# Second half of a fused decoder's attention: one visit of ScalarE for both query tiles of a head

## The chip, the cores and the metric

The kernel runs on one core of one Trainium2 chip. The metric is the device time of one execution in microseconds (us). The kernel before takes 2956.78 us, the median of three runs (2955.54 to 2959.35).

## The reference, cut to what matters

A two-layer decoder trunk over 512 tokens of width 1024. Layer 0 mixes gated linear attention and a dilated attention of 8 heads; layer 1 mixes by a recurrent block; after each mixer comes a mixture of 16384 one-neuron experts, of which every token takes 128. All is float32.

```
def reference(x, ...):
    h = x
    for layer in range(2):
        hn = rms_norm(h, mix_norm[layer])
        h = h + (gla_dilated_mixer(hn, ...) if layer == 0 else rglru_mixer(hn, ...))
        hn = rms_norm(h, ffn_norm[layer])
        h = h + peer_ffn(hn, ...)          # 128 rows of u and of v gathered for each token
    return rms_norm(h, final_norm)
```

The dilated attention of a head is computed as one masked softmax: the scores of the query rows over all keys up to them, plus a bias table that holds the penalties of the three branches, then exponentials, their sum, and the product with V, divided by the sum.

## The kernel before, in words

The 512 tokens are worked in two halves of 256, and the experts in eight passes p of 128 tokens (four for each layer). A pass has 128 slots k, one for each expert of a token. In slot k GpSimd issues one gather (1 MB: for each of 128 tokens an 8 KB row that holds u and v) into one of seven ring buffers (`pool`, L279); VectorE multiplies the u half by the token's row and sums it (`dot`, L296); ScalarE takes the Gelu of it (L301), weighs it by the gate (L309) and writes it on a diagonal (`place`, L313, three buffers); TensorE multiplies the diagonal by the v half and adds it up in PSUM (`sum_rows`, L346). Only then is the ring buffer free for the gather seven slots on.

Every other piece of work is spread over the slots by hand: each engine's program is a loop over k, and at the slots named there it issues, behind its own expert work of that slot, the instructions of the mixers, of the choice of the experts of the next pass, and so on. Engines execute in program order, so a piece that waits holds up everything behind it on its engine.

The second half's attention (g=1, called tile 1 here) lies in pass 1, from slot 4 (`ATT_AT`) to slot 42. It has 16 units u: head h = u // 2, query tile tl = u % 2; the even unit has 384 keys, the odd one 512. A unit goes through: scores on TensorE (L744, bank x % 2); bias and row maximum on VectorE (L955), then its scaled negative (L959); exponentials on ScalarE (L843); transposes of the 128-column blocks on TensorE (L752, 3 or 4 of them, one bank); their copy to SBUF on ScalarE (`keep`, L853, two buffers pT); the product with V on TensorE (L760); the reciprocal and the scaled result on VectorE (L963, L966). Before, one unit starts in every second slot: TensorE has the scores of u, the transposes of u-1 and the product of u-2 in slot 4+2u; VectorE has the bias of u and the result of u-2 in slot 8+2u; ScalarE has the exponentials of u and the keep of u-1 in slot 8+2u. The Gelu of the slots and the exponentials use different function tables of ScalarE, and a table is loaded (ACT_TABLE_LOAD) wherever the one follows the other. `Copy`, which the keep, the gates and the diagonals use, needs none.

Other work in these slots: the experts' choice on VectorE (L150 to L230) between slots 12 and 30, and bias tables of 256 KB loaded by SyncE (L641), one for each head into two buffers. The output projection of the mixer starts in slot 50 (`OUT_AT`), with its transposes in slot 46. The other half's attention (g=0) runs before the experts with the same functions.

Of the kernel before, what the change touches and what calls it, by code (L numbers as in the profile page):

```python
# [11 lines left out]
ALU = mybir.AluOpType  # L12
# [3 lines left out]
P = 128  # L16
D = 1024
KD = D // P
T = 512
# [7 lines left out]
GV_W = GH * GDV  # L27
# [529 lines left out]
class First:  # L557
# [170 lines left out]
    def sums(self, g):  # L728
        return self.ps[:, 3 if g else 7, 0:AHD]

    def att_pe(self, pe, g, u):

        nc, n = self.nc, 2 * AH
        if u == 0 and g:
            pe.wait_ge(self.gla_done, g + 1)
            pe.wait_ge(self.w.taken, self.FIRST[g] + self.IN)
        if u in (0, AH):
            pe.wait_ge(self.w.taken, self.until(g, 5 if u else 2))
        if u < n:
            h, tl, t, x = self.unit(g, u)  # L740
            r = slice(AHD * (h % 2), AHD * (h % 2) + AHD)
            if u >= 1 + g:
                pe.wait_ge(self.biased, x - g)
            nc.tensor.matmul(self.raw(g, x, t), self.aq[r, h // 2, tl * P:(tl + 1) * P],  # L744
                             self.ak[r, h // 2, 0:(t + 1) * P], start=True, stop=True).then_inc(self.qk_done, 1)
        if 1 <= u <= n:
            h, tl, t, x = self.unit(g, u - 1)
            pe.wait_ge(self.prob, x + 1)
            if u - 1 >= 1:
                pe.wait_ge(self.kept, x)  # L750
            for k in range(t + 1):
                last = nc.tensor.transpose(self.turned(g, x, t)[:, k * P:(k + 1) * P], self.pr[:, x % 2, k * P:(k + 1) * P], self.ident[:])  # L752
            last.then_inc(self.p_turned, 1)
        if u >= 2:
            h, tl, t, x = self.unit(g, u - 2)
            pe.wait_ge(self.kept, x + 1)
            if u > 2:
                pe.wait_ge(self.av_taken, x)
            for k in range(t + 1):
                last = nc.tensor.matmul(self.sums(g), self.pT[:, x % 2, k * P:(k + 1) * P],  # L760
                                        self.av[:, k, h * AHD:(h + 1) * AHD], start=k == 0, stop=k == t)
            last.then_inc(self.av_done, 1)
# [181 lines left out]

    def att_dve(self, dve, g, u):

        nc, scale = self.nc, float(AHD) ** -0.5
        if u < 2 * AH:
            h, tl, t, x = self.unit(g, u)
            w = (t + 1) * P  # L950
            dve.wait_ge(self.bias_in[h % 2], 16 * (g * AH // 2 + h // 2 + 1))
            dve.wait_ge(self.qk_done, x + 1)
            if u >= 2:
                dve.wait_ge(self.prob, x - 1)
            nc.vector.tensor_tensor_reduce(out=self.sc[:, x % 2, 0:w], in0=self.raw(g, x, t), in1=self.bias[:, h % 2, T - w:T],  # L955
                                           scale=1.0, scalar=NEG, op0=ALU.add, op1=ALU.max,
                                           accum_out=self.mx[:, x:x + 1]).then_inc(self.biased, 1)
            dve.wait_ge(self.biased, x + 1)
            nc.vector.tensor_scalar(self.nb[:, x:x + 1], self.mx[:, x:x + 1], -scale, None, ALU.mult).then_inc(self.neg, 1)  # L959
        if u >= 2:  # L960
            h, tl, t, x = self.unit(g, u - 2)
            dve.wait_ge(self.prob, x + 1)
            nc.vector.reciprocal(self.rden[:, x:x + 1], self.den[:, x:x + 1]).then_inc(self.recip, 1)  # L963
            dve.wait_ge(self.recip, x + 1)
            dve.wait_ge(self.av_done, x + 1)
# [292 lines left out]
ATT_AT = 4  # L1258
# [543 lines left out]
```

## Time and profile before

| | us |
|---|---|
| three runs, median | 2956.78 |
| profiled execution, its own time | 2957.95 |
| profiled execution, span from the first to the last instruction | 2956.2 |
| DMA, mean rate over the span | 400 GB/s |
| VectorE busy | 65% |
| ScalarE busy | 44% |
| TensorE matmul busy | 76% |
| mean granted TensorE clock | 0.852 |

The profile of one execution gives a page (busy time of the engines, the span in 40 slices, the DMA queues, the chain of work that ended last, the costliest groups of instructions) and answers to queries: a timeline of one engine, busy time in chosen stretches, groups of instructions with what ended the idle time before them. In a timeline a row is: start in us, length in us, engine, line of the kernel, operation, written and read tiles with shapes, count of merged instructions, and in brackets the idle time before it and who ended it.

### The profile page before, as it was taken

Reading aid. Unit: us, or ns where it says so; the run is one execution under the profiler, and the core shown is the slowest. Engines: PE = TensorE matmul, PEld = TensorE weight load, DVE = VectorE, ACT = ScalarE, POOL = GpSimd, SP = SyncE. Lnnn points to the kernel's source line nnn. Section 1 sums busy time; section 2 is a strip of 40 time slices with the busy share of each in tenths; the row PEclk is TensorE's granted clock in tenths of the full one; section 3 lists DMA queues with packets and bytes.
Section 4 is the critical chain, followed back from the end, with each engine's and each line's share of the span. In section 5 each row is a group of like instructions: output and inputs, shape, how many; then the busy total and the mean of one; then the engine's idle time right before and its main releaser. Section 6 shows DMA issues by size and latency. Waiting matters only on the chain.

```text
span 2956.2 us, 36171 instructions
## 1 busy us (share of the span) xinstructions
PE 2250.5 (76%) x12024; PEld 885.4 (30%) x12024; DVE 1908.4 (65%) x5677; ACT 1287.1 (44%) x3747; POOL 986.7 (33%) x1028
## 2 busy tenths in 40 slices
PE   8998898788896767778886776878787666756766
PEld 6773343233342222223332221323333111111110
DVE  1247757777477867576578666667478666567444
ACT  3233534485345438334343538433434333335333
POOL 0013333333333333333333333333333333333332
PEclk9999999889997988988998888979998766576666
DMA  5269999999999999999999999999999999999998
GB/s 187 104 233 426 426 426 427 422 369 404 427 426 423 398 427 407 427 426 426 427 426 426 412 427 397 422 425 426 426 426 419 416 427 427 427 415 426 427 426 338
DMA packets 166954, 1182.44 MB, mean 400 GB/s; under 512 B 19552, under 2 KB 20080, under 8 KB 24176
## 3 DMA queue, kind: packets, MB, share of 16 engines
q0 software_dynamic: 147456, 1073.81, 86.8%
q1 hardware_dynamic: 19312, 106.34, 9.0%
q8 instruction: 94, 1.54, 0.2%
q14 instruction: 92, 0.75, 0.1%
HBM read 1177.98 MB, written 2.10 MB: 399 GB/s over the span
## 4 chain that ended last, share of the span: by engine, by line
DMA 51%; PE 21%; DVE 13%; ACT 10%; issue 5%; POOL 0%; DVEq 0%; SPq 0%; ACTq 0%; POOLq 0%
DMA main_ring<-in_uv,main_idi 51%; PE main_bank L346 10%; DVE main_ring L296 6%; PE main_bank L384 4%; PE main_bank L382 4%; ACT main_diagonal L313 2%; ACT main_act_out L309 2%; ACT L301 1%; ACT main_act_out L301 1%; DVE main_topi L161 1%; DVE main_work L153 1%; DVE main_topi L155 1%; DVE main_resid L327 1%; DVE main_idf L208 1%; DVE main_top L150 1%
## 5 line engine op out<-in xcount | busy, mean ns | idle before, releaser
L346 PE MATMUL main_bank<-main_ring,main_diagonal 64*64 64x512 f32 x8192 | 1370.2, 755 | 620.6 <-ACT main_diagonal L313 578.8
L296 DVE CUSTOM_DVE_ANT_0 main_ring<-main_ring,main_bank 128x1024 f32<-128x1024 f32 x1024 | 1242.9, 1219 | 851.9 <-DMA main_ring<-in_uv,main_idi 842.5
L279 POOL DMA_INDIRECT main_ring<-in_uv,main_idi x1024 | 986.5, 963 | 1945.0 <-PE main_bank L346 1710.2
L301 ACT ACTIVATE main_act_out<-main_hid 128x1 f32<-128x1 f32 x1024 | 206.7, 202 | 1443.5 <-DVE main_hid L296 1442.3
L346 PEld LDWEIGHTS main_bank<-main_ring,main_diagonal 64*64 64x64 f32 x8192 | 254.6, 153 | 1407.5 <-ACT main_diagonal L313 1235.5
L384 PE MATMUL main_bank<-main_xT,main_w_block 128*128 128x256 f32 x1408 | 402.9, 414 | 5.7 <-ACT main_xT L417 5.7
L313 ACT ACTIVATE main_diagonal<-main_ones,main_act_out 128x64 f32<-128x64 f32 x1024 | 356.2, 348 | 39.5 <-PE main_bank L346 6.3
L384 PEld LDWEIGHTS main_bank<-main_xT,main_w_block 128*128 128x128 f32 x1408 | 250.4, 196 | 286.4 <-issue 253.5
L309 ACT ACTIVATE main_act_out<-main_act_out,main_gate 128x1 f32<-128x1 f32 x1024 | 301.6, 294 | 33.3
L384 PE MATMUL main_bank<-main_xT_query,main_w_block 128*128 128x256 f32 x512 | 135.2, 402 | 2.8 <-ACT main_xT L417 1.8
L384 PEld LDWEIGHTS main_bank<-main_xT_query,main_w_block 128*128 128x128 f32 x512 | 92.2, 193 | 76.7 <-issue 63.3
L301 ACT ACT_TABLE_LOAD x82 | 105.2, 1283 | 1.5
L382 PE MATMUL main_bank<-main_w_block,main_xT 128*128 128x256 f32 x384 | 102.8, 405 | 0.0
L382 PEld LDWEIGHTS main_bank<-main_w_block,main_xT 128*128 128x128 f32 x384 | 69.9, 195 | 50.5 <-issue 43.2
L296 DVE DVE_READ_ACCUMULATOR2_ANT main_hid<- 128x1 f32 x1024 | 84.2, 82 | 0.0
L382 PE MATMUL main_bank<-main_w_block,main_a_gate 128*128 128x256 f32 x256 | 75.7, 420 | 0.0
L382 PE MATMUL main_bank<-main_w_block,main_mixT 128*128 128x256 f32 x256 | 66.1, 409 | 1.6 <-ACT main_mixT L858 1.6
L382 PEld LDWEIGHTS main_bank<-main_w_block,main_a_gate 128*128 128x128 f32 x256 | 45.3, 197 | 59.3 <-issue 55.4
L201 DVE TENSOR_TENSOR main_pick<-main_pick,main_cand_id 128x800 f32<-128x800 f32 x64 | 60.6, 987 | 0.5
L195 DVE TENSOR_TENSOR main_pick<-main_posf,main_cand_at 128x800 f32<-128x800 f32 x64 | 60.5, 985 | 0.1
L208 DVE TENSOR_REDUCE main_idf<-main_pick 128x16 f32<-128x800 f32 x64 | 60.0, 978 | 0.1
L382 PEld LDWEIGHTS main_bank<-main_w_block,main_mixT 128*128 128x128 f32 x256 | 49.5, 201 | 26.3 <-issue 17.2
(196 smaller groups left out, 1252.7 us busy)
## 6 DMA issues: line engine op xcount, KB each, us to landing
main_w_block<-in_w_query SPq DMA_DIRECT2D x32, 1024.0 KB, 9.2
main_w_block<-in_w_ab SPq DMA_DIRECT2D x24, 1024.0 KB, 9.4
main_ring<-in_uv,main_idi POOLq DMA_INDIRECT x1024, 13.5
main_w_block<-in_w_c_in SPq DMA_DIRECT2D x16, 1024.0 KB, 9.2
main_w_block<-in_w_out SPq DMA_DIRECT2D x8, 1024.0 KB, 7.2
main_w_block<-in_w_c_out SPq DMA_DIRECT2D x8, 1024.0 KB, 9.4
main_att_bias<-in_att_bias SPq DMA_DIRECT2D x16, 256.0 KB, 4.9
main_keys<-in_keysT SPq DMA_DIRECT2D x2, 1024.0 KB, 18.5
```

The source lines that it names most:

```text
L150: last = nc.vector.max(best[:, low], values)
L195: last = self.nc.vector.tensor_tensor(self.pick[k][:], pos, at, ALU.is_equal)
L201: last = self.nc.vector.tensor_tensor(self.pick[k][:], self.pick[k][:], ids, ALU.mult)
L208: last = nc.vector.tensor_reduce(self.idf[:, k * PK:(k + 1) * PK], self.pick[k][:], AX.X, ALU.add)
L279: nc.gpsimd.indirect_dma_start(self.ring[n % self.bufs], None, self.uv[p // NT], bass.IndirectOffsetOnAxis(self.choice.idi[:, p % 2, k:k + ...
L296: self.nc.vector.tensor_tensor_reduce(out=row, in0=row, in1=self.ps[:, 6:8], scale=1.0, scalar=0.0, op0=ALU.mult, op1=ALU.add, accum_out=s ...
L301: self.nc.scalar.activation(self.act_out[:, k:k + 1], self.hid[:, k:k + 1], ACT.Gelu_apprx_tanh).then_inc(self.gelued, 1)
L309: self.nc.scalar.activation(weight, weight, ACT.Copy, scale=self.choice.gate[:, p % 2, k:k + 1]).then_inc(self.weighed, 1)
L313: self.nc.scalar.activation(self.diagonal[:, n % DIAGS], self.ones[:], ACT.Copy, scale=weight).then_inc(self.placed, 1)
L346: last = self.nc.tensor.matmul(self.ps[a * SIDE:(a + 1) * SIDE, 4 + r], self.diagonal[rows, n % DIAGS], self.ring[n % self.bufs][rows, D + ...
L382: last = nc.tensor.matmul(out, xT[:, d, cols], w[:, d], start=d == 0, stop=d == KD - 1)
L384: last = nc.tensor.matmul(out, w[:, d, cols], xT[:, d], start=d == 0, stop=d == KD - 1)
```

## The change

The functions `att_pe` and `att_dve` are cut into their steps, so that the steps can be placed apart. For g=0 the order of the instructions and their waits stay as they were. For g=1 the work now goes by heads, a head every four slots, with at = k - 4 - 4h:

- TensorE: scores of both units at 0; transposes of the even unit at 5, of the odd one at 7; both products with V at 9 (in the code ahead of the next head's transposes of the same slot). The product of the odd unit goes into the second 64 columns of the bank.
- VectorE: bias and maximum of the even unit at 2, of the odd one at 3; both results at 11, after both products are done.
- ScalarE: exponentials of both units at 4, one behind the other; keep of the even unit at 6, of the odd one at 8. In a slot where one head's keep meets the next head's exponentials, the keep goes first.

```diff
-    def sums(self, g):
-        return self.ps[:, 3 if g else 7, 0:AHD]
+    def sums(self, g, x):
+        return self.ps[:, 3, x % 2 * AHD:(x % 2 + 1) * AHD] if g else self.ps[:, 7, 0:AHD]
...
+    def att_turn_pe(self, pe, g, u):
+        h, tl, t, x = self.unit(g, u)
+        pe.wait_ge(self.prob, x + 1)
+        if u >= 1:
+            pe.wait_ge(self.kept, x)
...
+    def att_sum_pe(self, pe, g, u):
+        h, tl, t, x = self.unit(g, u)
+        pe.wait_ge(self.kept, x + 1)
+        if u > g * (u % 2):
+            pe.wait_ge(self.av_taken, x - g * (u % 2))
...
+    def att_out_dve(self, dve, g, u):
...
+        dve.wait_ge(self.av_done, x + 1 + g * (1 - u % 2))
...
-                        u = (k - ATT_AT - 4) // 2
-                        if k % 2 == 0 and 0 <= u < 2 * AH:
-                            mix0.att_exp_act(act, 1, u)
-                        if k % 2 == 0 and 0 < u <= 2 * AH:
-                            mix0.att_keep_act(act, 1, u - 1)
+                        for h in range(AH):
+                            at = k - ATT_AT - 4 * h
+                            if at in (6, 8):
+                                mix0.att_keep_act(act, 1, 2 * h + at // 8)
+                        for h in range(AH):
+                            if k == ATT_AT + 4 * h + 4:
+                                mix0.att_exp_act(act, 1, 2 * h)
+                                mix0.att_exp_act(act, 1, 2 * h + 1)
...
-                        u = (k - ATT_AT - 4) // 2
-                        if k % 2 == 0 and 0 <= u < 2 * AH + 2:
-                            mix0.att_dve(dve, 1, u)
+                        for h in range(AH):
+                            at = k - ATT_AT - 4 * h
+                            if at == 11:
+                                mix0.att_out_dve(dve, 1, 2 * h)
+                                mix0.att_out_dve(dve, 1, 2 * h + 1)
+                            if at in (2, 3):
+                                mix0.att_bias_dve(dve, 1, 2 * h + at - 2)
...
-                        u = (k - ATT_AT) // 2
-                        if k % 2 == 0 and 0 <= u < 2 * AH + 2:
-                            mix0.att_pe(pe, 1, u)
+                        for h in range(AH):
+                            at = k - ATT_AT - 4 * h
+                            if at == 9:
+                                mix0.att_sum_pe(pe, 1, 2 * h)
+                                mix0.att_sum_pe(pe, 1, 2 * h + 1)
+                            if at == 0:
+                                mix0.att_qk_pe(pe, 1, 2 * h)
+                                mix0.att_qk_pe(pe, 1, 2 * h + 1)
+                            if at in (5, 7):
+                                mix0.att_turn_pe(pe, 1, 2 * h + at // 7)
```

## Rows read from the trace of the kernel before

**Rows 1.** The page: DMA busy in tenths, the span in 40 slices.

```profile
DMA  5269999999999999999999999999999999999998
```

**Rows 2.** Busy time in the attention stretch and behind it; columns in the first line.

```profile
core 0: us, PE busy (x) PEld busy (x) DVE busy (x) ACT busy (x) POOL busy (x), PEclk, DMA share, GB/s
586.00:688.00 102.00, 80.25 (x492) 36.31 (x492) 74.11 (x249) 88.01 (x187) 33.54 (x36) 0.87 0.97 369
688.00:740.00 52.00, 44.35 (x253) 20.32 (x246) 40.51 (x141) 22.37 (x69) 18.89 (x20) 0.90 1.01 426
```

**Rows 3.** Groups of instructions, 586 to 688: busy us, mean ns | idle before them.

```profile
L279 POOL DMA_INDIRECT main_ring<-in_uv,main_idi x36 | 33.7, 936 | 70.0 <-PE main_bank L346 65.7 <-issue 4.3
L301 ACT ACT_TABLE_LOAD x16 | 20.5, 1283 | 0.3
L843 ACT ACT_TABLE_LOAD x15 | 19.2, 1283 | 0.3
...
L752 PE MATMUL main_bank<-main_ident,main_att_p 128*128 128x128 f32 x56 | 9.6, 289 | 20.8 <-ACT main_att_pT L853 17.9 <-ACT main_att_p L843 2.9
```

**Rows 4.** Timeline of ScalarE, single steps and the first and last exponentials.

```profile
585.74 0.35 ACT L313 ACTIVATE main_diagonal<-main_ones,main_act_out 128x64 f32<-128x64 f32 x1
...
587.40 0.61 ACT L843 ACTIVATE main_att_p<-main_att_s,main_att_nb 128x384 f32<-128x384 f32 x1
...
589.41 0.20 ACT L301 ACTIVATE main_act_out<-main_hid 128x1 f32<-128x1 f32 x1
...
589.98 0.35 ACT L313 ACTIVATE main_diagonal<-main_ones,main_act_out 128x64 f32<-128x64 f32 x1
...
592.76 0.72 ACT L843 ACTIVATE main_att_p<-main_att_s,main_att_nb 128x512 f32<-128x512 f32 x1
593.39 0.19 ACT L843 ACTIVATION_READ_ACCUMULATOR main_att_p<-main_att_s,main_att_nb 128x1 f32 x1
...
623.21 0.57 ACT L853 ACTIVATE main_att_pT<-main_bank 128x512 f32<-128x512 f32 x1
...
629.27 0.47 ACT L853 ACTIVATE main_att_pT<-main_bank 128x384 f32<-128x384 f32 x1
...
676.31 0.72 ACT L843 ACTIVATE main_att_p<-main_att_s,main_att_nb 128x512 f32<-128x512 f32 x1
```

**Rows 5.** Timeline of TensorE: expert rows, transposes and products, at either clock.

```profile
576.40 1.09 PE L346 MATMUL main_bank<-main_ring,main_diagonal 64*64 64x512 f32 x8 [0.85 <-ACT main_diagonal L313]
...
581.28 1.98 PE L346 MATMUL main_bank<-main_ring,main_diagonal 64*64 64x512 f32 x8 [0.41 <-ACT main_diagonal L313]
...
588.16 0.90 PE L752 MATMUL main_bank<-main_ident,main_att_p 128*128 128x128 f32 x3 [2.89 <-ACT main_att_p L843]
...
599.99 0.52 PE L752 MATMUL main_bank<-main_ident,main_att_p 128*128 128x128 f32 x3 [1.72 <-ACT main_att_pT L853]
600.34 1.00 PE L760 MATMUL main_bank<-main_att_v,main_att_pT 128*128 128x64 f32 x8
...
605.91 0.63 PE L752 MATMUL main_bank<-main_ident,main_att_p 128*128 128x128 f32 x4 [0.19 <-ACT main_att_pT L853]
606.37 0.78 PE L760 MATMUL main_bank<-main_att_v,main_att_pT 128*128 128x64 f32 x6
...
611.79 1.57 PE L760 MATMUL main_bank<-main_att_v,main_att_pT 128*128 128x64 f32 x8
```

**Rows 6.** Timeline of VectorE: dots of slots 12, 19 and 44, a bias.

```profile
593.69 1.22 DVE L296 CUSTOM_DVE_ANT_0 main_ring<-main_ring,main_bank 128x1024 f32<-128x1024 f32 x1 [1.23 <-DMA main_ring<-in_uv,main_idi]
...
613.67 0.69 DVE L955 CUSTOM_DVE_ANT_0 main_att_s<-main_bank,main_att_bias 128x512 f32<-128x512 f32 x1
...
614.91 1.22 DVE L296 CUSTOM_DVE_ANT_0 main_ring<-main_ring,main_bank 128x1024 f32<-128x1024 f32 x1
...
688.17 1.22 DVE L296 CUSTOM_DVE_ANT_0 main_ring<-main_ring,main_bank 128x1024 f32<-128x1024 f32 x1 [1.78 <-DMA main_ring<-in_uv,main_idi]
```

**Rows 7.** Gathers of line 279 from issue to landing, 586 to 688.

```profile
DMA to landing us min/median/max: 5.4/8.3/13.2
```

More of the change, by code:

```diff
@@ L738, in att_pe @@
             pe.wait_ge(self.w.taken, self.until(g, 5 if u else 2))
-        if u < n:
[L740 to L745, printed above, removed]
-        if 1 <= u <= n:
[L747 to L753, printed above, removed]
@@ L754, in att_pe @@
-        if u >= 2:
[L755 to L762, printed above, removed]
+        h, tl, t, x = self.unit(g, u)
+        r = slice(AHD * (h % 2), AHD * (h % 2) + AHD)
@@ new lines, in att_qk_pe @@
+        if u >= 1 + g:
+            pe.wait_ge(self.biased, x - g)
+        self.nc.tensor.matmul(self.raw(g, x, t), self.aq[r, h // 2, tl * P:(tl + 1) * P],
+                              self.ak[r, h // 2, 0:(t + 1) * P], start=True, stop=True).then_inc(self.qk_done, 1)
+    def att_turn_pe(self, pe, g, u):
[3 more added lines that the diff above has]
+            pe.wait_ge(self.kept, x)
+        for k in range(t + 1):
+            last = self.nc.tensor.transpose(self.turned(g, x, t)[:, k * P:(k + 1) * P], self.pr[:, x % 2, k * P:(k + 1) * P], self.ident[:])
+        last.then_inc(self.p_turned, 1)
@@ new lines, in att_sum_pe, with att_pe @@
+    def att_sum_pe(self, pe, g, u):
+        h, tl, t, x = self.unit(g, u)
+        pe.wait_ge(self.kept, x + 1)
+        if u > g * (u % 2):
+            pe.wait_ge(self.av_taken, x - g * (u % 2))
+        for k in range(t + 1):
+            last = self.nc.tensor.matmul(self.sums(g, x), self.pT[:, x % 2, k * P:(k + 1) * P],
+                                         self.av[:, k, h * AHD:(h + 1) * AHD], start=k == 0, stop=k == t)
+        last.then_inc(self.av_done, 1)
+    def att_pe(self, pe, g, u):
+        n = 2 * AH
+        if u < n:
+            self.att_qk_pe(pe, g, u)
+        if 1 <= u <= n:
+            self.att_turn_pe(pe, g, u - 1)
+        if u >= 2:
+            self.att_sum_pe(pe, g, u - 2)
@@ L943, in gla_scale_dve, with att_bias_dve @@
         self.link(dve, nc.vector.tensor_tensor(o, o, self.head_gain[:].unsqueeze(1).to_broadcast([P, 2, GV_W]), ALU.mult))
+    def att_bias_dve(self, dve, g, u):
+        h, tl, t, x = self.unit(g, u)
+        w = (t + 1) * P
+        dve.wait_ge(self.bias_in[h % 2], 16 * (g * AH // 2 + h // 2 + 1))
+        dve.wait_ge(self.qk_done, x + 1)
+        if u >= 2:
+            dve.wait_ge(self.prob, x - 1)
+        self.nc.vector.tensor_tensor_reduce(out=self.sc[:, x % 2, 0:w], in0=self.raw(g, x, t), in1=self.bias[:, h % 2, T - w:T],
+                                            scale=1.0, scalar=NEG, op0=ALU.add, op1=ALU.max,
+                                            accum_out=self.mx[:, x:x + 1]).then_inc(self.biased, 1)
+        dve.wait_ge(self.biased, x + 1)
+        self.nc.vector.tensor_scalar(self.nb[:, x:x + 1], self.mx[:, x:x + 1], -float(AHD) ** -0.5, None, ALU.mult).then_inc(self.neg, 1)
@@ L945, in att_dve @@
     def att_dve(self, dve, g, u):
-        nc, scale = self.nc, float(AHD) ** -0.5
         if u < 2 * AH:
[L949 to L959, printed above, removed]
@@ L960, in att_dve @@
[L960 to L968 removed]
+            self.att_bias_dve(dve, g, u)
@@ L971 @@
+        if u >= 2:
+            self.att_out_dve(dve, g, u - 2)
 class Recurrent:
```

13 lines of the change are left out of this document (8 added, 5 removed).

## The prediction

> **What bounds the kernel now.** I read the page first, for what the whole run lives on: the DMA engines are busy nine tenths or more of every slice from the fourth on [rows 1]. The gathers are the work that can't be hidden; where an engine keeps the ring from being refilled, DMA time is lost for good. Next I read the busy time by stretch. Behind the attention (688 to 740) DMA moves 426 GB/s, in the attention (586 to 688) 369 [rows 2]. At 426 the bytes of the 102 us would have taken 102 x 369 / 426 = 88.4 us, so at most some 13.6 us are lost there. The same row says who is busy: ScalarE 88.0 of 102 us, VectorE 74.1, TensorE 80.3. Then the groups of instructions: GpSimd waits 65.7 us for TensorE to free a ring buffer, TensorE waits for ScalarE's keep and exponentials, and ScalarE spends 20.5 + 19.2 us on 31 table loads of 1.283 us [rows 3]. A thirty-second load stands before an exponential of the experts' choice that shares slot 28 with an attention unit. So ScalarE sets the pace: its first exponential starts at 587.40 and its last at 676.31 [rows 4], 15 units in 88.91 us, 5.93 a unit and 11.85 us a head of four slots. The work of the four slots themselves is 4 x 0.82 (Gelu at 589.41, end of the diagonal at 590.33, less the overlap with the next), four loads 5.13, exponentials 0.62 + 0.72, keeps 0.47 + 0.57: 10.8 us, and about 1 us of waits.
>
> What could be won: slot 12 starts at 593.69 and slot 44 at 688.17, each as soon as its gather is there [rows 6]. That is 94.5 us for 32 slots. At 426 GB/s a gather of 1.05 MB takes 2.46 us and a bias table (0.26 MB, some six of them) 0.6, so 32 x 2.46 + 3.7 = 82.4: 12.1 us is the most the stretch can give back.
>
> **The change, part by part.** *Table loads.* A head needs one load for its two exponentials and one back for the Gelu, where it needed four: 16 loads fewer in the pass, 16 x 1.283 = 20.5 us of ScalarE, 2.57 a head. ScalarE's own work falls from 10.8 to 8.3 us a head, under the 9.8 + 0.6 us that DMA needs for four gathers and a bias table. If ScalarE's work alone were the limit, all 12 us would come back.
>
> Here the Trainium skill's page ScalarE: Activation LUTs (What ACT_TABLE_LOAD costs) gives every switch 1283 ns and about 1380 ns of drain besides. The first half agrees with the rows. The second doesn't show here, for the Gelu starts 1.29 us behind its load and the ten microseconds and a bit above already fill the head; by the page's 2.66 us the saving would be 5.3 us a head. The measured 1.28 decides.
>
> *The handing to and fro.* What was a pipeline over units has become one chain inside a head, because of where the steps stand in the programs of two engines that execute in order. Call K the end of the odd keep of the head before, in the slot at 4, and follow what must come one after the other (full TensorE clock):
>
> 1. ScalarE: load 1.29, exponentials 0.62 + 0.82 (the second with the accumulator read at 593.39 that must end before a load), load 1.29, then Gelu, weight and diagonal of the slot at 5, 0.92 [rows 3, 4]: 4.94.
> 2. TensorE has this slot's expert rows first, 1.14 from the diagonal's end (L313 to the end of the 1.09 us group) [rows 5]: 6.08. Behind them stand the two products of the head before, 0.71 and 0.94 to the next start (1.00 and 0.78 us groups, overlapping the next), and only then the even transposes, 0.52 [rows 5]: 8.25, and 0.13 to reach ScalarE: 8.38.
> 3. ScalarE, which has done slot 6 by 5.8 and stands at the even keep, is released: keep 0.47, then slot 7's diagonal 0.92 [rows 4]: 9.8.
> 4. TensorE: slot 7's rows 1.14, odd transposes 0.63, 0.13 to reach ScalarE [rows 5]: 11.7.
> 5. ScalarE: odd keep 0.57 [rows 4]: 12.27; two overlaps of 0.07 between TensorE groups come off: 12.2 us.
>
> So ScalarE waits 2.5 us at the even keep and about 1 us at the odd one, which is more than the 2.57 us that it no longer loads. The head takes 12.2 us where it took 11.85. This chain doesn't depend on the ring, so no amount of landed gathers helps it.
>
> VectorE hangs on it but doesn't lengthen it: its two results in slot 7 wait for both products (done at about K + 7.9), then come results and odd bias, 0.4 more than the 1.24 us of one bias and one result [rows 6], and slot 8's dot 1.2: K + 10.8, and ScalarE's slot 8 ends at 11.7, when the transposes do. That the products share a bank, so that the first result waits for the second product too, costs 0.9 us of VectorE wait and nothing on the chain.
>
> *Clock.* The granted clock in the stretch is 0.87 [rows 2], so TensorE has 1.2 GHz for 26% of it. At 1.2 GHz the rows take 1.98 instead of 1.09, three transposes 0.90 for 0.52, eight product matmuls 1.57 for 1.00 [rows 5]. Over the chain's TensorE steps (two groups of rows 1.8 more, products 1.1, transposes 0.8) a head fully at 1.2 GHz would take 3.7 us more. The stretch's first 5 us were slow throughout (the transposes at 588.16 [rows 5]); that leaves (0.26 x 102 - 5) / 97 = 22% for the rest, and 22% of 3.7 is 0.8. Before, 1 us of TensorE idle each unit hid most of this; on the new chain nothing does. I take 0.8: P = 13.0 us a head. Bounds: 12.2 (the slow stretches fall on the scores or on idle time), and 13.9 (one slow stretch begins with every head's burst).
>
> *Start.* The diagonal of slot 8 ends at 586.09, now as before [rows 4]. The first head has no products ahead of its transposes; at 1.2 GHz for slot 9, as before at that time [rows 5]: +4.94 = 591.0, rows 2.03, transposes 0.90 + 0.13, keep 0.47, diagonal 0.92, rows and odd transposes 1.90, keep 0.57: K = 598.0. Six more heads: K7 = 598.0 + 6 P = 676.0 before the last exponentials.
>
> *End.* The price is read where DMA is fed again, slot 44. There the change gives something back: TensorE stood two slots behind ScalarE (its transposes of a unit were placed two slots ahead of the unit's exponentials), now it follows at once. Behind the last exponentials slot 38's rows end at K7 + 9.2 (rows of 37, products, transposes, rows of 38). That frees the buffer of slot 45, whose gather lands 5.5 us later at the quickest [rows 7]: K7 + 14.9 with the issue, so slot 44 is due at K7 + 12.4 at the full rate. 676.0 + 12.4 = 688.4, against 688.17 [rows 6]. The sum is +0.2 us. With P = 12.2 it is 671.2 + 12.4 = 683.6, -4.6 us; with 13.9 it is 693.8, +5.6.
>
> *The rest.* Bias tables: a buffer is freed in slot 4h-5 and needed in 4h+2, seven slots where there were six, so they stay hidden. The scores wait for nothing new: both banks are free once the head before has its biases. GpSimd's and SyncE's programs are unchanged. The final results move from slot 42 to 43, ahead of the transposes in slot 46: nothing. Instructions of g=0 are the same.
>
> **The rivals.** *A, ScalarE's time is what counts.* If ScalarE's waits at the keeps are much shorter than my chain says (half of the transposes' latency overlapped, say), P falls under 12 and toward the 10.4 that DMA needs. For it: ScalarE is the busiest engine and loses a quarter of its work. Against: every step of the chain is a wait in program order. At P = 11.5 slot 44 comes at 679.4, -8.8 us (2949.2); the end is -12.1 (2945.9). It counts as faster from P = 12.0 down.
>
> *B, the slow clock joins the chain.* TensorE now stands still while ScalarE runs loads and exponentials (idle from about K + 3 to K + 5), then has its whole burst on the chain. If each burst falls at 1.2 GHz, P = 12.2 + 1.7 to 12.2 + 3.7. It is slower beyond the bound from P = 13.95; at 14.3 slot 44 comes at 696.2, +8.0 us (2966). For it: at 581 the clock fell and the rows behind took 1.98 us, after TensorE had idled between single slots [rows 5]. Against: before, TensorE idled too, 20.8 us ahead of its transposes [rows 3], and had 0.87.
>
> The skill's page TensorE: Matmul & The Clock Gate (HAM oscillation) says that waits between bursts send the array back to half rate and that the next burst starts slow; by it B would be the rule.
>
> *C, the loads are not merged* (something between the two exponentials calls the other table, or the keep needs one). Nothing between them is a Gelu, and the keeps beside an exponential had no load of their own [rows 3]. It would add 2.57 a head to P: slower by 15 us. I give it 1 in 50.
>
> **How the numbers follow.** Profiled execution 2957.95 us, median 2956.78, 1.2 lower; the sum +0.2 is put on the median: 2957.0. Forecast (chain as written, P from 12.0 to 13.95): 60%. A 23%, B 15%, C 2%. The measurement can tell about 0.2%, 5.9 us, from no change; so faster 23%, same 60%, slower 17%. The forecast's own range is 2951 to 2963; to leave out no more than 2 in 10 it reaches halfway into A: 2947.5, and a little into B: 2964.
>
> **What would show it.** In the profile after: 16 table loads fewer in pass 1; ScalarE idle ahead of L853's keeps, ended by the transposes, some 2.5 us at the even and 1 at the odd unit, about 25 us in all; exponential pairs 12.2 to 13.9 us apart; TensorE's rows end within 3 us of their diagonal instead of 6; DMA in the stretch still under 426 GB/s; slot 44's dot at 684 to 694. I am wrong if the pairs are under 12 us apart (A), if the rows and products stand at their 1.2 GHz lengths in nearly every head (B), or if another engine ends ScalarE's idle time, VectorE above all in slots 12 to 26, where the choice of experts lies on it.

## The result, and the profile after

The changed kernel takes 2971.05 us (median of five runs, 2970.47 to 2976.88) against 2956.78 for the kernel before: 1.0046 times as long, 95% interval 1.0035 to 1.0056. It is 14.3 us slower. The profiled execution took 2970.63 us, 12.7 more than that of before.

The page after, the lines that answer to [rows 1], with the clock (tenths of full speed):

```profile
span 2968.7 us, 36154 instructions
...
PEclk9999999978898878979998797979999766666666
DMA  5269999989999999999999999999999999999998
```

The busy time by stretch, as in [rows 2]:

```profile
core 0: us, PE busy (x) PEld busy (x) DVE busy (x) ACT busy (x) POOL busy (x), PEclk, DMA share, GB/s
586.00:688.00 102.00, 79.84 (x393) 36.04 (x393) 65.95 (x228) 61.32 (x147) 28.73 (x30) 0.77 0.90 336
688.00:740.00 52.00, 46.04 (x266) 22.50 (x267) 38.32 (x137) 21.18 (x73) 20.24 (x21) 0.84 0.93 377
```

In the attention stretch DMA moves 336 GB/s where it moved 369, and behind it 377 instead of 426. (426 - 336) x 102 + (426 - 377) x 52 is 11.7 MB, 27.5 us of DMA at 426; before it was 13.6. The difference, 13.9 us, is as large as the whole loss. ScalarE is busy 61 us instead of 88, so the loads did go; TensorE's granted clock fell from 0.87 to 0.77.

Groups of instructions from 586 to 688 (busy us, mean ns | idle before them), as in [rows 3]; L852 are now the exponentials, L862 the keeps, L973 the results:

```profile
L279 POOL DMA_INDIRECT main_ring<-in_uv,main_idi x30 | 28.7, 958 | 73.6 <-PE main_bank L346 72.4 <-issue 1.2
...
L862 ACT ACTIVATE main_att_pT<-main_bank 128x384 f32<-128x384 f32 (+1 forms) x14 | 7.6, 542 | 33.1 <-PE main_bank L750 33.0
...
L301 ACT ACT_TABLE_LOAD x8 | 10.3, 1283 | 0.1
...
L852 ACT ACT_TABLE_LOAD x7 | 9.0, 1283 | 0.1
...
L973 DVE TENSOR_SCALAR main_mixed<-main_bank,main_att_rden 128x64 f32<-128x64 f32 x12 | 3.4, 284 | 25.0 <-PE main_bank L759 24.7
```

Fifteen loads stand in the stretch instead of 31 (the head in slot 28 shares one with the choice of the experts, as before). In exchange ScalarE stands 33.0 us ahead of its keeps until the transposes come; before, it didn't wait there at all. Two of the sixteen keeps lie behind 688; with them it is 40.5 us. GpSimd waits 72.4 us for TensorE to free a buffer (65.7 before).

One head on ScalarE, with what it waits for:

```profile
597.78 0.60 ACT L862 ACTIVATE main_att_pT<-main_bank 128x512 f32<-128x512 f32 x1 [1.50 <-PE main_bank L750]
...
599.69 0.61 ACT L852 ACTIVATE main_att_p<-main_att_s,main_att_nb 128x384 f32<-128x384 f32 x1
...
602.97 0.35 ACT L313 ACTIVATE main_diagonal<-main_ones,main_act_out 128x64 f32<-128x64 f32 x1
...
608.94 0.49 ACT L862 ACTIVATE main_att_pT<-main_bank 128x384 f32<-128x384 f32 x1 [4.82 <-PE main_bank L750]
...
612.23 0.60 ACT L862 ACTIVATE main_att_pT<-main_bank 128x512 f32<-128x512 f32 x1 [0.30 <-PE main_bank L750]
```

From the end of the odd keep at 598.38 to that at 612.83 it is 14.45 us. Between the odd keeps of the eight heads lie seven such distances, 14.45, 15.82, 14.45, 16.04, 10.51, 14.44 and 16.03. In this head the even keep waits 4.82 us; the sum had 2.5. The same stretch on TensorE (the products are L759, the transposes L750):

```profile
603.38 1.71 PE L346 MATMUL main_bank<-main_ring,main_diagonal 64*64 64x512 f32 x8 [2.92 <-ACT main_diagonal L313]
605.02 3.25 PE L759 MATMUL main_bank<-main_att_v,main_att_pT 128*128 128x64 f32 x14
608.06 0.85 PE L750 MATMUL main_bank<-main_ident,main_att_p 128*128 128x128 f32 x3
608.84 1.91 PE L346 MATMUL main_bank<-main_ring,main_diagonal 64*64 64x512 f32 x8
```

Every step of the chain is there in the order foretold: rows, both products, even transposes, and only then the keep. But products and transposes have their 1.2 GHz length, 3.25 us for 14 product matmuls and 0.85 for the transposes. The rows, 1.71, lie between their two lengths, 1.09 and 1.98: the clock fell while they ran. Ahead of them TensorE had been idle for 2.92 us. So it is in six of the seven heads: behind 2.64 to 4.61 us of idle time the products take 3.25. In three of the six the rows are slow from their start (1.98 or 1.99), in the other three the clock falls inside them (1.71, 1.28, 1.31). One head ran otherwise, the one in slot 28. There the exponential of the experts' choice has loaded the table ahead of the keep, so ScalarE's double visit is one load shorter and TensorE is idle for half as long:

```profile
662.71 1.09 PE L346 MATMUL main_bank<-main_ring,main_diagonal 64*64 64x512 f32 x8 [1.49 <-ACT main_diagonal L313]
663.73 1.77 PE L759 MATMUL main_bank<-main_att_v,main_att_pT 128*128 128x64 f32 x14
665.34 0.50 PE L750 MATMUL main_bank<-main_ident,main_att_p 128*128 128x128 f32 x3
```

Here all is at full speed, products 1.77, transposes 0.50. This head took 10.5 us from odd keep to odd keep, and 1.3 of load ahead of the keep, 11.8: the full-clock sum of the prediction was 12.2.

### The profile page after: what moved, and what is told of

Same layout as the page of the kernel before. It is cut to its first block, busy times and chain, and to the rows that moved or that the text cites. A ratio compares the mean times of both kernels' runs of the same rounds, so it can differ in the third digit from the quotient of the medians.

```text
span 2968.7 us, 36154 instructions
## 1 busy us (share of the span) xinstructions
PE 2261.6 (76%) x12024; PEld 892.0 (30%) x12024; DVE 1907.5 (64%) x5677; ACT 1267.0 (43%) x3731; POOL 989.8 (33%) x1028
## 4 chain that ended last, share of the span: by engine, by line
DMA 50%; PE 22%; DVE 13%; ACT 9%; issue 5%; POOL 0%; DVEq 0%; SPq 0%; POOLq 0%; ACTq 0%
DMA main_ring<-in_uv,main_idi 50%; PE main_bank L346 12%; DVE main_ring L296 6%; PE main_bank L384 4%; PE main_bank L382 3%; ACT main_diagonal L313 2%; ACT main_act_out L309 2%; ACT L301 1%; ACT main_act_out L301 1%; PE main_bank L759 1%; DVE main_topi L161 1%; DVE main_work L153 1%; DVE main_resid L327 1%; DVE main_topi L155 1%; DVE main_idf L208 1%
## 5 line engine op out<-in xcount | busy, mean ns | idle before, releaser
L313 ACT ACTIVATE main_diagonal<-main_ones,main_act_out 128x64 f32<-128x64 f32 x1024 | 356.2, 348 | 33.5
## 6 DMA issues: line engine op xcount, KB each, us to landing
main_ring<-in_uv,main_idi POOLq DMA_INDIRECT x1024, 13.5
```

The source lines that it names most:

```text
L313: self.nc.scalar.activation(self.diagonal[:, n % DIAGS], self.ones[:], ACT.Copy, scale=weight).then_inc(self.placed, 1)
```

## Experiments

The theory: the chain of the prediction is right, and TensorE's half clock in every burst behind ScalarE's double visit is what makes a head 14.3 instead of 12 us. Rivals: the visit itself, 4 us in which ScalarE makes no diagonal, starves TensorE whatever the order; VectorE's wait for both products (the shared bank) holds back the dots; ScalarE's load sets the pace after all. "K distance" below is the time between the ends of odd keeps of two heads, 14.5 us in the mean of the changed kernel's seven; a burst is what TensorE does in one go behind its idle time: rows, products, transposes. All were timed in turn with the kernel before on the same chip, and a ratio is to that kernel's time there.

**1. The products at 8.**

```diff
-                            if at == 9:
+                            if at == 8:
                                 mix0.att_sum_pe(pe, 1, 2 * h)
                                 mix0.att_sum_pe(pe, 1, 2 * h + 1)
```

> One part of the changed kernel moved: TensorE's two products with V stand at 8 of a head instead of 9, that is while ScalarE has the next head's loads and exponentials. My theory (a chain of waits between ScalarE and TensorE inside a head, lengthened by the slow clock that TensorE's idle time brings): the products leave the chain, 1.7 us at full and 3.2 us at half clock a head, and TensorE's idle time before the burst shrinks from 2.9 us to under 1.5, so the clock stays up. Odd keeps end about 10.8 us apart instead of 14.5; time 2946 to 2955 us, faster than before. Rival 1 (the long double visit of ScalarE itself starves the ring): nothing changes, 2965 to 2972. Rival 2 (VectorE's wait for both products of a bank): its waits vanish too, so it gives the same as mine here and is told apart by the products-behind-turns run.

Measured: 2949.58 us (2945.54 to 2951.21), ratio 0.9973 (0.9963 to 0.9984). With one digit changed the kernel is 21 us faster than the changed one and 7 faster than before. The products now stand ahead of the idle time, and TensorE's busy row of the stretch and one head of its timeline are:

```profile
586.00:688.00 102.00, 83.17 (x514) 33.97 (x507) 81.15 (x284) 70.03 (x182) 37.24 (x40) 0.90 1.00 411
```

```profile
631.70 1.77 PE L759 MATMUL main_bank<-main_att_v,main_att_pT 128*128 128x64 f32 x14
633.40 1.77 PE L741 MATMUL main_bank<-main_att_k,main_att_q 64*128 64x384 f32 x4
636.38 1.09 PE L346 MATMUL main_bank<-main_ring,main_diagonal 64*64 64x512 f32 x8 [1.21 <-ACT main_diagonal L313]
637.40 0.55 PE L750 MATMUL main_bank<-main_ident,main_att_p 128*128 128x128 f32 x3
```

The idle time is 1.21 us, rows and transposes are at full length 1.09 and 0.55, the stretch's clock 0.90, DMA 411 GB/s. K distances run from 8.8 to 13.6, mean 11.2, instead of 14.5. This speaks against the visit as a cost in itself, since the double visit is unchanged. It doesn't part the order from the clock, for both changed here; run 5 does that.

**2. The products behind the even transposes, in the same slot.**

```diff
-                            if at == 9:
-                                mix0.att_sum_pe(pe, 1, 2 * h)
-                                mix0.att_sum_pe(pe, 1, 2 * h + 1)
...
                             if at in (5, 7):
                                 mix0.att_turn_pe(pe, 1, 2 * h + at // 7)
+                        for h in range(AH):
+                            if k - ATT_AT - 4 * h == 9:
+                                mix0.att_sum_pe(pe, 1, 2 * h)
+                                mix0.att_sum_pe(pe, 1, 2 * h + 1)
```

> One order changed: in the slot at 9 TensorE does the next head's even transposes first and the two products behind them. My theory: only part of the products leaves the chain, because the even keep writes the buffer that the even product reads and waits for it; the odd product goes, 0.94 us at full and 1.9 at half clock a head, so 7 to 13 us less than the changed kernel: 2958 to 2965 us. If the keep's wait for the buffer didn't count, it would be as with the products at 8 (2946 to 2955). If VectorE's wait for both products were the cost, the products here end later than in the changed kernel and the time would be 2971 or more.

Measured: 2964.91 us (2961.01 to 2967.83), ratio 1.0027 (1.0016 to 1.0038), 6.1 us under the changed kernel; K distance 13.6 in the mean. Even keeps now wait for a product, not for transposes:

```profile
632.03 0.49 ACT L862 ACTIVATE main_att_pT<-main_bank 128x384 f32<-128x384 f32 x1 [3.06 <-PE main_bank L759]
```

So the keep's wait for its buffer counts, as was said, and it is not enough to let the transposes go first. Against what was expected, VectorE's results did not come later here: they start 9.6 to 9.8 us behind the odd keep in most heads, 9.6 to 10.3 in the changed kernel. So this run says nothing against VectorE as the cause; run 3 has to. What it does show is a new wait: VectorE stands until both products are done, with a dot behind it, and ScalarE waits for that dot, 15.1 us from 586 to 688 where it was 5.4:

```profile
635.57 0.20 ACT L301 ACTIVATE main_act_out<-main_hid 128x1 f32<-128x1 f32 x1 [2.26 <-DVE main_hid L296]
```

**3. VectorE's results at 12.**

```diff
-                            if at == 11:
+                            if at == 12:
                                 mix0.att_out_dve(dve, 1, 2 * h)
                                 mix0.att_out_dve(dve, 1, 2 * h + 1)
```

> The changed kernel with one step of VectorE moved: both results stand at 12 of a head instead of 11, behind the dot of the slot in which ScalarE has its double visit. VectorE waited 38 us for the products in the changed kernel, with dots behind it. My theory: that wait is not what sets the pace, since ScalarE waits for TensorE in the same slot; 2967 to 2972 us, at most 0.8 us a head less. Rival (VectorE's wait for both products, which came with the shared bank, holds the dots back and is the cost): 2952 to 2962 us.

Measured: 2972.07 us (2971.05 to 2975.16), ratio 1.0051 (1.0037 to 1.0064): no change against 1.0046. VectorE's waits for the products, 24.7 us ahead of its results in the changed kernel, are 12.1 here, and nothing is won by it. In the order of the changed kernel the shared bank is cleared; in that of run 2 it was not tested.

**4. Two visits again.**

```diff
                             if k == ATT_AT + 4 * h + 4:
                                 mix0.att_exp_act(act, 1, 2 * h)
+                            if k == ATT_AT + 4 * h + 5:
                                 mix0.att_exp_act(act, 1, 2 * h + 1)
```

> One part undone: the two exponentials of a head go in two visits again, the odd one a slot later, with two more table loads a head (16 in all, 20.5 us of ScalarE). My theory: the added loads fall into ScalarE's wait for the even transposes, and the first visit is shorter by 0.7 us, so the chain gets no longer: 2960 to 2973 us. Rival (ScalarE's load sets the pace, and the change's saving was real but offset): 2985 to 2993 us.

Measured: 2966.34 us (2962.69 to 2969.06), ratio 1.0029 (1.0018 to 1.0041). Sixteen more loads, 20.5 us of ScalarE, and the kernel is 4.7 us faster than with one visit; K distance 13.6 in the mean. (The intervals of the two ratios just overlap; the single runs don't, 2969.06 at most here and 2970.47 at least there.) The loads lie in time that ScalarE would wait, and the first diagonal of a burst is done 0.7 us sooner. In the head whose burst starts at 631.50 TensorE's idle time is 2.21 us instead of 2.92, and in three of the heads the clock falls only inside the products, which take 2.8 to 2.9 us instead of 3.25. The saving that the change brought was worth nothing where it was brought.

**5. Work for TensorE in its idle time.** Behind the scores two products of the identity with 512 columns go into the transposes' bank; nobody reads them, so the kernel computes what it did and more.

```diff
+    def fill_pe(self, pe, g, u):
+        h, tl, t, x = self.unit(g, u)
+        pe.wait_ge(self.kept, x + 1)
+        for k in range(2):
+            self.nc.tensor.matmul(self.turned(g, x, 3), self.ident[:], self.ak[:, k, 0:T], start=True, stop=True)
...
+                        for h in range(AH):
+                            if k - ATT_AT - 4 * h == 8:
+                                mix0.fill_pe(pe, 1, 2 * h + 1)
```

> The changed kernel with work added: behind the scores, where TensorE is idle 2.9 us a head, it does two more 128x512 products of the identity into the transposes' bank, that nobody reads (some 1.7 us at full clock). My theory (the half clock of the burst behind the idle time is what makes a head 14.5 instead of 12.2 us): the idle time falls under 1.5 us, the burst runs at full clock, odd keeps end about 12.2 us apart, and the kernel gets faster by adding work: 2954 to 2961 us. Rival (the clock is no cause, the chain is longer for another reason): 2970 or more.

Measured: 2956.29 us (2953.51 to 2959.65), ratio 0.9998 (0.9988 to 1.0007). TensorE has eight times 1.98 us more to do and the kernel is 14.8 us faster. A head of its timeline (L777 are the added products), the last row the next head's burst:

```profile
622.19 1.77 PE L741 MATMUL main_bank<-main_att_k,main_att_q 64*128 64x384 f32 x4
623.89 1.98 PE L777 MATMUL main_bank<-main_att_k,main_ident 128*128 128x512 f32 x4
626.61 1.09 PE L346 MATMUL main_bank<-main_ring,main_diagonal 64*64 64x512 f32 x8 [0.73 <-ACT main_diagonal L313]
627.63 1.77 PE L759 MATMUL main_bank<-main_att_v,main_att_pT 128*128 128x64 f32 x14
629.24 0.50 PE L750 MATMUL main_bank<-main_ident,main_att_p 128*128 128x128 f32 x3
...
638.54 1.09 PE L346 MATMUL main_bank<-main_ring,main_diagonal 64*64 64x512 f32 x8 [0.73 <-ACT main_diagonal L313]
```

Between the same rows of two heads lie 638.54 - 626.61 = 11.93 us, and every step is at full speed: the chain with the clock taken out, foretold at 12.2. Six of the seven heads have their products at 1.77 us. Their K distances are 11.9 to 12.2, but for 10.5 in the head with the shared load and 13.5 in the one before it, in which that load stands. The last head, for which no scores are left to do, has 2.43 us of idle time, products of 3.25 and a K distance of 15.95. That the total, 2956.3, is so near to the prediction's 2957.0 is in part chance: the heads took 12.0 us in the mean of the prediction's six, for which its sum gives 2951, and the last one was slow again.

**6 and 7. The wait alone, and half the work.** The same with the loop's body left out (`range(0)`), and with one product (`range(1)`).

> Control for the filled kernel: the changed kernel with the filled kernel's added wait (TensorE waits behind the scores for the odd keep) and without its added products. Theory (the added work kept TensorE's clock up): without the work nothing is left, odd keeps 14.5 us apart, 2968 to 2974 us. Rival (the wait reordered something that helped): 2955 to 2960, as the filled kernel.

Measured: 2973.73 us (2969.56 to 2978.08), ratio 1.0055 (1.0041 to 1.007). The wait brings nothing; a burst behind 3 us of idle time again:

```profile
648.40 1.36 PE L346 MATMUL main_bank<-main_ring,main_diagonal 64*64 64x512 f32 x8 [3.01 <-ACT main_diagonal L313]
649.69 3.25 PE L759 MATMUL main_bank<-main_att_v,main_att_pT 128*128 128x64 f32 x14
```

> The filled kernel with one added product a head instead of two, so TensorE's idle time ahead of the burst is about 2 us instead of 1.2 (full clock) or 2.9 (none). Theory: the clock is the cause, so the time follows it, whichever way it goes here: with odd keeps about 12 us apart and the slow share near 0.2 it is 2954 to 2960 us; with 14.5 and near 0.5 it is 2968 to 2973; heads of both kinds give a time between. Rival: time and clock don't go together.

Measured: 2958.80 us (2953.17 to 2964.87), ratio 1.0005 (0.9996 to 1.0014). K distances are 11.94 in two heads of seven, 10.5 in the one with the shared load and 13.5 to 16.0 in the others, mean 13.1. Only two heads have slow products, with 16.0 and 14.5; the two of 13.5 and 13.6 have theirs at full speed, and in one of them stands the choice's load. The share of time at 1.2 GHz from 586 to 704 is 0.22, against 0.49 in the changed kernel and 0.20 in the filled one; heads with slow products are two, six and one of seven, and all seven with the wait alone. The totals go with the clock in all four. The single runs of this kernel spread over 12 us, but so did those of the kernel before beside it (2952.5 to 2964.3), so the spread says nothing.

**8. TensorE's steps at 4 and 6, keeps at 5 and 7, products at 8.**

```diff
-                            if at in (6, 8):
-                                mix0.att_keep_act(act, 1, 2 * h + at // 8)
+                            if at in (5, 7):
+                                mix0.att_keep_act(act, 1, 2 * h + at // 7)
...
-                            if at in (5, 7):
-                                mix0.att_turn_pe(pe, 1, 2 * h + at // 7)
+                            if at in (4, 6):
+                                mix0.att_turn_pe(pe, 1, 2 * h + at // 6)
```

(The products stand at 8 besides, as in run 1.)

> The changed kernel with the handing to and fro taken apart: products at 8, and the transposes at 4 (even, right behind the exponentials of the same slot) and 6 (odd) instead of 5 and 7, the keeps at 5 and 7 instead of 6 and 8. So each keep finds its transposes done before ScalarE comes to it. My theory: ScalarE's waits ahead of the keeps, 67.5 us in the changed kernel and 42.9 with the products at 8 alone, mostly go; a head takes what DMA or VectorE need, 10 to 11 us; slot 44's gather lands at 676 to 679 us, and the time is 2943 to 2950 us, at or up to 6 us under the run with the products at 8. Rival (a double visit of ScalarE starves TensorE whatever the order): no better than products at 8, 2949 or more, with ScalarE's idle time moved to another wait.

Measured: 2951.30 us (2948.69 to 2953.70), ratio 0.9975 (0.9965 to 0.9984): just over the range I gave, no better than run 1. ScalarE's wait ahead of its keeps did go (11.6 us from 586 to 688, 33 in the changed kernel), but five of seven heads took 9.3 to 11.0 us and two took 19.6 and 15.1. In the first of these VectorE is busy with the choice of experts (slots 12 and 15), ScalarE waits 4.2 us for a dot, TensorE is idle for 4.52 and its burst slow:

```profile
609.26 1.98 PE L346 MATMUL main_bank<-main_ring,main_diagonal 64*64 64x512 f32 x8 [4.52 <-ACT main_diagonal L313]
611.18 3.25 PE L759 MATMUL main_bank<-main_att_v,main_att_pT 128*128 128x64 f32 x14
```

Then VectorE waits for scores that stand behind this burst. What was expected of the order came; what the choice's work on VectorE does to it was left out of the sum. But the rival's signs came as well: no better than run 1, with ScalarE's wait moved elsewhere, to the dots (17.4 us in the stretch, 5.4 in the changed kernel). So this run doesn't rule out that the double visit has a small cost of its own.

**9. The kernel before with TensorE two slots later.** The other part of the change, done alone: without new visits, only TensorE no longer waits two slots back.

```diff
-                        u = (k - ATT_AT) // 2
+                        u = (k - ATT_AT - 2) // 2
                         if k % 2 == 0 and 0 <= u < 2 * AH + 2:
                             mix0.att_pe(pe, 1, u)
```

> The kernel before with one step changed: TensorE has a unit's scores, transposes and product two slots later (6+2u instead of 4+2u), so it doesn't stand two slots back waiting for the exponentials. All table loads are kept. My theory of the kernel before: ScalarE's own work, 10.8 us a head, set its pace, with 1 us of waits; TensorE's lag kept two of the seven ring buffers from GpSimd. The lag goes: a head takes 10.8 to 11.5 us, DMA is fed again 3 to 8 us earlier: 2948 to 2955 us. Rival (ScalarE's load alone counts, the lag costs nothing): 2955 to 2958, no change.

Measured: 2949.20 us (2946.88 to 2950.39), ratio 0.9969 (0.9957 to 0.9981), 9.6 us faster than before, with all 32 loads in it. It is the lowest time of all runs, but not to be told from run 1 (0.9969 and 0.9973, and the intervals overlap). ScalarE's timeline, two units:

```profile
606.59 0.62 ACT L843 ACTIVATE main_att_p<-main_att_s,main_att_nb 128x384 f32<-128x384 f32 x1
...
607.21 0.58 ACT L853 ACTIVATE main_att_pT<-main_bank 128x512 f32<-128x512 f32 x1
...
612.12 0.72 ACT L843 ACTIVATE main_att_p<-main_att_s,main_att_nb 128x512 f32<-128x512 f32 x1
...
612.84 0.47 ACT L853 ACTIVATE main_att_pT<-main_bank 128x384 f32<-128x384 f32 x1
...
617.64 0.61 ACT L843 ACTIVATE main_att_p<-main_att_s,main_att_nb 128x384 f32<-128x384 f32 x1
```

617.64 - 606.59 is 11.05 us a head, and the same in all but the last within 0.2; in the kernel before it was 11.85 [rows 4]. ScalarE has no wait ahead of a keep, and had none in the kernel before. What went is another wait, the one for TensorE to free one of the three diagonals (L313). Before and here, from 586 to 688:

```profile
L313 ACT ACTIVATE main_diagonal<-main_ones,main_act_out 128x64 f32<-128x64 f32 x36 | 12.5, 348 | 7.2 <-PE main_bank L346 6.3
```

```profile
L313 ACT ACTIVATE main_diagonal<-main_ones,main_act_out 128x64 f32<-128x64 f32 x39 | 13.6, 348 | 1.3
```

Its own work was summed to 10.8. The stretch:

```profile
586.00:688.00 102.00, 81.61 (x521) 35.43 (x521) 82.58 (x293) 88.14 (x195) 35.57 (x38) 0.92 1.01 411
```

DMA moves 411 GB/s instead of 369. The clock is 0.92 instead of 0.87, and how much of the gain is the clock's was not parted from the order's.

**10 and 11. More room for every hand-over, with one visit and with two.** Keeps at 7 and at 8 behind the next exponentials, products at 10, results at 12.

```diff
+                        for h in range(AH):
+                            at = k - ATT_AT - 4 * h
+                            if at in (7, 8):
+                                mix0.att_keep_act(act, 1, 2 * h + at // 8)
...
-                            if at == 11:
+                            if at == 12:
...
-                            if at == 9:
+                            if at == 10:
```

(The keeps' loop at 6 and 8 ahead of the exponentials is gone. The second kernel has the odd exponentials at 5 besides, as in run 4.)

> The changed kernel with every hand-over given a slot or two of room: even keep at 7 instead of 6, odd keep at 8 behind the next head's exponentials instead of ahead of them, products at 10 and results at 12 instead of 9 and 11; transposes stay at 5 and 7, the exponentials in one visit. My theory: the chain is 5.5 (load, exponentials, odd keep, load, diagonal) + 1.1 (rows) + 0.7 (transposes), 7.3 us, by which time ScalarE has only just come to the even keep, so ScalarE hardly waits for TensorE and a head takes DMA's 10.4 us: 2943 to 2950 us. Rival (one visit for both exponentials costs by itself, by the 4 us in which no diagonal is made): 2955 or more, as with the changed order before.

Measured: 2950.25 us (2948.09 to 2955.07), ratio 0.9978 (0.9969 to 0.9987), K distances 10.3 in three heads, 8.8 in one and 13.0 to 14.5 in three. Again no better than products at 8 or than run 9, with half of run 9's loads. The time lies just over the range of the theory (2950) and under that of the rival (2955).

> The same with the odd exponential in a visit of its own at 5, so with two more table loads a head (32 in pass 1 as in the kernel before). Here nothing hides them: ScalarE's work is 10.8 us a head instead of 8.3, just over DMA's 10.4. My theory: 1 to 5 us more than the run with one visit, that is the real worth of the change's merging: small, because DMA is behind it at once. Rival (16 loads of 1.28 us are worth their 20.5 us when ScalarE doesn't wait for TensorE): 15 us or more. Rival 2 (the visits' shorter blocks help TensorE's clock and the ring): less than the run with one visit.

Measured: 2971.48 us (2969.73 to 2975.58), ratio 1.0050 (1.0037 to 1.0064), 21 us more than with one visit. That is outside what I expected, and the size is by chance that of sixteen loads. The rival's reason isn't borne out: it needs a ScalarE that doesn't wait, and here it waits 21 us from 586 to 688 ahead of its keeps (15.6 with one visit), and K distance is 14.4 to 15.4 where its own work is 10.8. The stretch points at the clock:

```profile
586.00:688.00 102.00, 85.67 (x390) 37.54 (x383) 64.11 (x224) 77.94 (x158) 26.68 (x28) 0.70 0.87 332
```

The clock is 0.70, the lowest of all runs (0.60 of the time from 586 to 704 at 1.2 GHz, 0.29 with one visit). The products are slow in all seven heads, in two with one visit. So I had left the clock out of a sum once more. That it is the whole of the 21 us is argued, not shown: this order was not run with TensorE's idle time filled. What a table load is worth on a ScalarE that never waits stays open: no order here had both one visit and no waits, so it wasn't measured.

## Why the prediction was wrong

The likeliest case, no measurable change at 2957.0 us, did not come; the time lies above the range (2964), on the side of rival B, which had 15% and a price of +8 us.

- **What bounds the kernel: right, and incomplete.** DMA starves in the stretch, and ScalarE sets the pace there. Run 9, which only moves TensorE's steps, brought a head from 11.85 to 11.05 us and the kernel down by 9.6 us; ScalarE's 6.3 us of waiting for diagonals went with it. The prediction counted TensorE's lag only as something that the change gives back at the end.
- **Loads: right.** Sixteen went, 20.5 us. The prediction said they would pay if ScalarE's work alone were the limit; run 4 put them back and lost nothing.
- **The chain: right, step by step.** 12.2 us at full clock (its own figures add up to 12.1); 11.9 in the filled kernel, 11.8 in the one undisturbed head of the changed one. The order rows, products, transposes, keep is as written. ScalarE's wait at the keeps is there too, 40.5 us where the chain at full clock gave about 25, and 25.3 us in the filled kernel. That VectorE lengthens no head held (run 3).
- **The clock: the step that failed.** The sum took the stretch's share of slow time as it was before, 22%, and spread it evenly over the chain: 0.8 us a head. From 591 to 688 it is 48% after (granted clock 0.76), and it lies on the burst. From the odd keep that ends at 598.38 to this one it is six heads:

```profile
683.49 0.60 ACT L862 ACTIVATE main_att_pT<-main_bank 128x512 f32<-128x512 f32 x1 [0.70 <-PE main_bank L750]
```

684.09 - 598.38 = 85.71, so P, the time of one head, is 14.3 us where I had 13.0. Over the 12.2 at full clock the clock cost 2.1 us a head, not 0.8. The start, K = 598.0, was right within 0.4 us. P lies beyond 13.95, from where B was to show, and B's own reasoning (idle while ScalarE has its visit, then all work on the chain) is what happened, as is the sign that was named for it: products at their 1.2 GHz length in nearly every head. The row that I held against it, that TensorE had been idle before too, did not bear the argument: of its sixteen idle pieces ahead of transposes there, only the first (2.89 us) and one other (2.29) were longer than 1.8 us, most were 1.1 to 1.5, as in this row of the kernel before, and ScalarE had no wait at its keeps for the work behind them.

```profile
635.41 0.52 PE L752 MATMUL main_bank<-main_ident,main_att_p 128*128 128x128 f32 x3 [1.35 <-ACT main_att_pT L853]
```

A share of the time is no guide to a step that always comes behind the idle time. K7, the last of these odd keeps, came 8.1 us late, 0.4 of it from the start.
- **The end: the same term again.** I had the last burst at full clock, slot 38's rows done at K7 + 9.2. They end at about 696.8 here (the first half of the last group below, which holds the rows of two slots; a group of 8 alone takes 1.98), K7 + 12.7, 3.5 us later:

```profile
689.09 1.98 PE L346 MATMUL main_bank<-main_ring,main_diagonal 64*64 64x512 f32 x8 [4.61 <-ACT main_diagonal L313]
691.00 3.25 PE L759 MATMUL main_bank<-main_att_v,main_att_pT 128*128 128x64 f32 x14
694.04 0.85 PE L750 MATMUL main_bank<-main_ident,main_att_p 128*128 128x128 f32 x3
694.82 3.69 PE L346 MATMUL main_bank<-main_ring,main_diagonal 64*64 64x512 f32 x16
```

With both, 0.2 + 8.1 + 3.5 = 11.8 us; the profiled executions differ by 12.7, the medians by 14.3. The rest, 1 to 2.5 us, is not explained.
- **Slot 44, where the price was to be read.** Its dot was due at 688.4, by the range at 684 to 694, and came at 704.47:

```profile
703.87 0.28 DVE L973 TENSOR_SCALAR main_mixed<-main_bank,main_att_rden 128x64 f32<-128x64 f32 x1 [4.20 <-PE main_bank L759]
...
704.47 1.21 DVE L296 CUSTOM_DVE_ANT_0 main_ring<-main_ring,main_bank 128x1024 f32<-128x1024 f32 x1
```

That is 16.3 us behind the kernel before, more than was lost in all. VectorE stands 4.20 us ahead of this dot for the last head's products; the prediction had the last results' move to slot 43 at nothing. With the results a slot later (run 3) the same wait lies behind this dot, and the kernel is no faster. So slot 44's dot is not a good place to read the price.
- **The bookkeeping.** The times for A and B were reckoned from the profiled execution, 2957.95, and the forecast from the median, 2956.78. On the median B's 8.0 us make 2964.8, not 2966. No conclusion hangs on it.

The Trainium skill's page TensorE: Matmul & The Clock Gate (HAM oscillation) had the rule, that waits between bursts let the next one begin slow. These traces agree in the main: rows 1.98 us behind 4.5 us of idle time, 1.09 behind 1.2 and 1.5. Behind 2.92 us they differ from it in part, for in two of those four heads the rows began at full clock (1.71 and 1.28 in all) and only what followed was wholly slow. I gave the case that the page describes 15%, though I had worked out that the change makes such waits.

## What to carry to other kernels

Fewer table loads, or any lighter load of the busiest engine, buy nothing if the new order makes it wait inside the same period: write down the chain of hand-overs for one period before counting work, and leave a step of other work between an engine's product and the engine that takes it (runs 1, 8 and 10). Where a chain holds a burst of TensorE behind idle time of nearly 3 us, as here, price the burst at 1.2 GHz too; put independent TensorE work into the idle time rather than behind it. And look at what an engine waits for although its input can't be there yet: moving TensorE's steps two slots later, one number in the kernel before, brought as much as the best order found for the rewrite (2949.20 against 2949.58 us).

## What was not expected of the hardware

Two extra 128x512 float32 products a head, 1.98 us each pair, sixteen in all, took 14.8 us off the changed kernel, and one product a head took 12.3 off. TensorE at 1.2 GHz did the 14 product matmuls in 3.25 us and at 2.4 in 1.77. In the changed kernel they ran slow in the six heads whose burst came behind 2.64 to 4.61 us without work, and at full speed in the one with 1.49 us.
